# Attention denominators with tokens on partitions, and the last norm inside the feed-forward block

## The chip, the cores and the metric

The kernel runs on one core of one Trainium2 chip, in float32 carried through the matrix engine as pairs of high and low parts. The metric is device microseconds (us) of one execution. Before the change three runs gave a median of 2854.69 us (2854.20 to 2859.28). PE is the matrix engine (TensorE), DVE is VectorE, ACT is ScalarE, POOL is GpSimd, and SP issues most of the DMAs. PSUM is the accumulator memory that PE writes; SBUF is the on-chip memory that all engines share.

## The reference, cut to what matters

One encoder layer is applied to 512 + 1024 = 1536 tokens of width 1024:

- normalise, and one input projection to attention's q, k and v (8 query heads, 2 key heads, width 64), the mLSTM's q, k, v, o and gates, and two merge gates;
- attention in blocks of 512 queries: softmax over all keys of the token's own sequence, `o = sum(p * v) / sum(p)`, where p is the exponential of the score less the query's maximum;
- the mLSTM branch, the merge, the output projection, a norm and a residual, which give x1;
- the gated feed-forward part: `u = h @ w_up`, a convolution and gelu on one half, times the other half, `y = act @ w_down` (2816 to 1024), and last `x1 + rmsnorm(y, norm_ffn_post)`.

## The kernel before

The stages stand one after another, each a block in which every engine has its own list of instructions, ordered by semaphores. Every product of two float32 matrices is three matmuls (`mm3`, lines 77 to 79: high by high, high by low, low by high) of 128 x 128 by 128 x 512.

**Attention (`attention`).** A unit is one head's 512 queries; there are 24. A step is 256 keys of it: eight units have two steps and sixteen have four, 80 steps in all. All engines walk over the same slots, one per step, PE two steps ahead with the scores. In slot i PE does: part of the input projection (`project`, the filling work, about 14 matmuls in a slot); `turn_top` for the unit that starts three slots later; `weigh(i)`, the four products of probabilities and v; more projection; `scores(i+2)`, four matmuls; for a unit that ended in slot i-1, `sums`; and `piece`, products for the row maxima of the next unit, in between more projection. DVE does in slot i: `keep_lo(i+1)` (the low half of the probabilities, L819), then for a unit that ended in slot i-2 `invert` and `normalise`, for one that ends now `fold`, then the low half of a projection weight (L497), the maxima (`reduce`, L804 and L806; `top`, L815), and `add_halves`. POOL adds the probabilities up (L723). ACT takes the exponentials.

The denominators: `fold` leaves 128 x 512 partial sums, keys on partitions. `sums` multiplies them by a 128 x 128 matrix of ones into the bank pDen, which so holds each query's sum on every partition, and DVE takes the reciprocal of 64 x 512 of it (L842) and multiplies (L849). pDen is also where `turn_top` turns the maxima (128 tokens on partitions) into a row. So before it turns, PE waits for all reciprocals so far:

```python
for u in starting(i + 3):
    if sums_done:
        pe.wait_ge(inverted, sums_done)
    turn_top(u)
```

The pieces for the maxima go to the two banks of pM in turn.

**Feed-forward (`ffn`).** A loop runs over the 22 slices of 128 of the inner width. For each, PE makes the gate products, the down products of the slice before (12 token tiles of 128, two halves of 512 each), and the val products. DVE splits weights into halves, runs convolution and activation in three chunks of 512 tokens, and adds each down product to y_sum (L2072). After the last slice PE waits for all three chunks, and makes the last down products.

**Last norm (`final_norm`).** A block of its own behind the loop: per token tile ACT squares and sums y_sum (L2226) and takes the root (L2230), DVE takes the reciprocal (L2242), scales and multiplies by the gain (L2245, 128 x 1024), and adds x1 (L2250, 128 x 1024). SP loads x1 four tiles ahead and stores y.

Of the kernel before, what the change touches and what calls it, by code (L numbers as in the profile page):

```python
# [24 lines left out]
F32 = mybir.dt.float32  # L25
# [499 lines left out]
def attention(nc, k):  # L525

    with ExitStack() as ctx:
# [35 lines left out]
        ones = sb("att_ones", [P, P], F32R)  # L563
# [4 lines left out]
        o_half, o_sum, o_out = sb("o_half", [H2, CH]), sb("o_sum", [H2, CH]), sb("o_out", [H2, 2, CH])  # L568
        top2, tops = sb("att_top2", [P, 4, 2]), sb("att_tops", [P, 4, P])
        rinv = sb("att_rinv", [H2, CH])  # L570
# [4 lines left out]
        g_ones = sb("gate_ones", [R, 2 * CH])  # L575
# [14 lines left out]
        summed, inverted, normed = sem("p_summed"), sem("inverted"), sem("o_normed")  # L590
# [24 lines left out]
        def pieces_until(i):  # L615
            return sum(len(x) for x in PIECES[:i + LEAD])

# [7 lines left out]
        def _(sp):  # L625
# [47 lines left out]
            for i in slots():  # L673
# [14 lines left out]
                for u in ending(i - 2):  # L688
                    store_a(u)
# [36 lines left out]
        def _(act):  # L726
# [14 lines left out]
            def keep_top(u):  # L741
                act.wait_ge(m_turned, u + 1)
                act.wait_ge(q_in[u % 3], 48 * (u // 3 + 1))
                act.activation(q_m[H2:H2 + 1, u % 3, :], pD[H2:H2 + 1, :], ACT.Copy).then_inc(m_kept, 1)
# [50 lines left out]
        def _(dve):  # L795
            def reduce(u, p):
                n = KT[u] // 4
                qb, s = p // n, p % n
                at = BEGUN[u] + p
                dve.wait_ge(pieced, at + 1)  # L800
                if n == 1:
                    if u and p == 0:
                        dve.wait_ge(m_turned, u)
                    dve.tensor_reduce(tops[:, qb, H2:H2 + 1], pM[:, at % 2, :], AX_X, ALU.max).then_inc(reduced, 1)  # L804
                else:
                    dve.tensor_reduce(top2[:, qb, s:s + 1], pM[:, at % 2, :], AX_X, ALU.max).then_inc(reduced, 1)  # L806
# [25 lines left out]
            def add_halves(u):  # L832
                dve.wait_ge(halved, u + 1)
                if u:
                    dve.wait_ge(normed, u)
                dve.tensor_tensor(o_sum[:, :], pO[0:H2, :], o_half[:, :], ALU.add).then_inc(o_added, 1)

            def invert(u):
                dve.wait_ge(summed, u + 1)
                if u:  # L840
                    dve.wait_ge(normed, u)
                dve.reciprocal(rinv[:, :], pD[0:H2, :]).then_inc(inverted, 1)  # L842

            def normalise(u):
                dve.wait_ge(inverted, u + 1)
                dve.wait_ge(o_added, u + 1)
                if u >= 2:
                    dve.wait_ge(a_out[u % 2], 16 * (u // 2))
                dve.tensor_tensor(o_out[:, u % 2, :], o_sum[:, :], rinv[:, :], ALU.mult).then_inc(normed, 1)  # L849
# [39 lines left out]
            for i in slots():  # L889
                if i + 1 >= 0 and i + 1 < NS:  # L890
                    keep_lo(i + 1)
                for u in ending(i - 2):
                    invert(u)
                    normalise(u)
# [24 lines left out]
        def _(pe):  # L919
# [7 lines left out]
            def piece(u, p):  # L927
# [7 lines left out]
                if at >= 2:  # L935
                    pe.wait_ge(reduced, at - 1)
                k0 = SEG_OF_CHUNK[c][0] * P + s * CH
                pe.matmul(pM[:, at % 2, :], q_st[:, u % 3, qb * P:(qb + 1) * P], k_st[:, k0:k0 + CH],  # L938
                          start=True, stop=True).then_inc(pieced, 1)

            def turn_top(u):
                pe.wait_ge(topped, u + 1)
                for qb in range(4):
                    last = pe.transpose(pD[:, qb * P:(qb + 1) * P], tops[:, qb, :], k.ident[:, :])
                last.then_inc(m_turned, 1)
# [28 lines left out]
            def sums(u):  # L974
                pe.wait_ge(fold_split, u + 1)
                pe.matmul(pD[:, :], ones[:, :], s_hi[:, :], start=True, stop=False)
                pe.matmul(pD[:, :], ones[:, :], s_lo[:, :], start=False, stop=True).then_inc(summed, 1)
# [10 lines left out]
            tops_done = sums_done = 0  # L988
            for i in slots():
                due = DUE[i + LEAD]  # L990
                project(due - 2 * (due // 3))
                for u in starting(i + 3):
                    if sums_done:
                        pe.wait_ge(inverted, sums_done)
                    turn_top(u)
                    tops_done += 1
# [5 lines left out]
                for u in ending(i - 1):  # L1002
                    pe.wait_ge(m_kept, tops_done)
                    sums(u)
                    sums_done += 1
# [6 lines left out]
            sums(NU - 1)  # L1012
            pe.wait_ge(exped, 2 * NS)
# [916 lines left out]
def ffn(nc, k, h2_hi, h2_lo, y_sum):  # L1930
# [4 lines left out]
    with ExitStack() as ctx:  # L1935
# [5 lines left out]
        def sem(name):  # L1941
# [22 lines left out]
                                                            sem("act_h"), sem("act_l"), sem("y_summed"))  # L1964
        start_at_one(nc, used)
# [7 lines left out]
        last_f = NFF - 1  # L1973

# [5 lines left out]
        def _(sp):  # L1980
# [20 lines left out]
            with sp.Fori(1, NFF // 2) as i:  # L2001
                three(2 * i, 0)
                three(2 * i + 1, 1)

        @block.vector
        def _(dve):
# [91 lines left out]
            add_down(last_f)  # L2098

        @block.scalar  # L2100
        def _(act):
# [20 lines left out]
            with act.Fori(0, NFF) as f:  # L2122
                copy_gate(f)
                gelus(f)

        @block.tensor
        def _(pe):
# [42 lines left out]
            down_products(last_f)  # L2170

def final_norm(nc, k, y_sum):

    with ExitStack() as ctx:
        def sb(name, shape, dt=F32):
            return ctx.enter_context(nc.sbuf_tensor(name, shape, dt))

        used = []  # L2180

        def sem(name):
            used.append(ctx.enter_context(nc.semaphore(name)))
            return used[-1]

        RING = 4
        gain, x_t, y_t = sb("f_gain", [P, D]), sb("f_x1", [P, RING, D]), sb("f_y", [P, RING, D])
        squares, stat = sb("f_sq", [P, D]), sb("f_stat", [P, 3, RING])
        gain_in, x_in = sem("f_gain_in"), [sem(f"f_x1_in{b}") for b in range(RING)]
        squared, rooted, inverted, scaled, added = sem("f_squared"), sem("f_rooted"), sem("f_inverted"), sem("f_scaled"), sem("f_added")  # L2190
        out = [sem(f"y_out{b}") for b in range(RING)]
        start_at_one(nc, used)
        block = ctx.enter_context(nc.Block())

        def tiles(eng, body):
            with eng.Fori(0, NT // RING) as i:  # L2196
                for b in range(RING):
                    body(RING * i + b, b, i)

        @block.sync  # L2200
        def _(sp):
            sp.dma_start(gain[:, :], k.norm_ffn_post.partition_broadcast(P)).then_inc(gain_in, 16)
            for b in range(RING):
                sp.dma_start(x_t[:, b, :], k.x1[b * P:(b + 1) * P, :]).then_inc(x_in[b], 16)

            def store(t, b):
                sp.wait_ge(added, t + 2)
                sp.dma_start(k.y[bass.ds(t * P, P), :], y_t[:, b, :]).then_inc(out[b], 16)

            with sp.Fori(0, NT // RING - 1) as i:  # L2210
                for b in range(RING):
                    t = RING * i + b
                    store(t, b)
                    sp.dma_start(x_t[:, b, :], k.x1[bass.ds((t + RING) * P, P), :]).then_inc(x_in[b], 16)
            for b in range(RING):
                store(NT - RING + b, b)
            for b in range(RING):
                sp.wait_ge(out[b], 16 * (NT // RING) + 1)

        @block.scalar  # L2220
        def _(act):
            act.sem_inc(inverted, RING - 1)

            def statistics(t, b, i):
                act.wait_ge(rooted, t + 1)
                act.activation(squares[:, :], y_sum[:, bass.ds(t, 1), :].rearrange("p a n -> p (a n)"), ACT.Square,  # L2226
                               accum_out=stat[:, 0, b:b + 1]).then_inc(squared, 1)
                act.wait_ge(squared, t + 2)
                act.wait_ge(inverted, t + 1)
                act.activation(stat[:, 1, b:b + 1], stat[:, 0, b:b + 1], ACT.Sqrt, scale=1.0 / D,  # L2230
                               bias=k.eps[:, 0:1]).then_inc(rooted, 1)

            tiles(act, statistics)

        @block.vector
        def _(dve):
            dve.wait_ge(gain_in, 17)
            dve.wait_ge(inverted, RING)

            def finish(t, b, i):  # L2240
                dve.wait_ge(rooted, t + 2)
                dve.reciprocal(stat[:, 2, b:b + 1], stat[:, 1, b:b + 1]).then_inc(inverted, 1)  # L2242
                dve.wait_ge(inverted, t + RING + 1)  # L2243
                dve.wait_ge(out[b], 16 * i + 1)  # L2244
                dve.scalar_tensor_tensor(out=y_t[:, b, :], in0=y_sum[:, bass.ds(t, 1), :].rearrange("p a n -> p (a n)"),  # L2245
                                         scalar=stat[:, 2, b:b + 1], in1=gain[:, :],
                                         op0=ALU.mult, op1=ALU.mult).then_inc(scaled, 1)
                dve.wait_ge(scaled, t + 2)
                dve.wait_ge(x_in[b], 16 * (i + 1) + 1)  # L2249
                dve.tensor_tensor(y_t[:, b, :], y_t[:, b, :], x_t[:, b, :], ALU.add).then_inc(added, 1)  # L2250

            tiles(dve, finish)
# [46 lines left out]
def encoder_block(nc, x, norm_mix_pre, w_in, b_if, q_norm, k_norm, mlstm_norm_w, w_attn_o, w_mlstm_o, w_out,  # L2299
# [18 lines left out]
    with ExitStack() as ctx:  # L2318
# [22 lines left out]
        with ExitStack() as second:  # L2341
# [4 lines left out]
            final_norm(nc, k, y_sum)  # L2346
# [41 lines left out]
```

## Time and profile before

| | |
|---|---|
| median of three runs | 2854.69 us |
| profiled execution | 2859.45 us |
| its span, first to last instruction | 2857.6 us |
| PE busy | 2483.2 us (87%) |
| DVE busy | 1786.3 us (63%) |
| ACT busy | 885.8 us (31%) |
| POOL busy | 497.1 us (17%) |
| mean granted TensorE clock | 0.934 |

The busy time of an engine counts its instructions and not the waits before them. A group of instructions names its line, its engine, what it writes and reads, its count, its busy time and the mean of one, and the idle time of its engine just before such instructions with what ended it. A granted clock of 1.0 is 2.4 GHz and 0.5 is 1.2 GHz. A matmul's duration contains its run through the pipeline; what it costs in a stream is the distance from start to start.

### The profile page before, as it was taken

What the parts mean: (1) busy time and instruction counts of PE and PEld (TensorE: products, weight loads), DVE (VectorE), ACT (ScalarE), POOL (GpSimd) and SP (SyncE); (2) the same over time, 40 slices, a digit from 0 to 9 for tenths busy, and PEclk for the clock granted to TensorE, in tenths of its full rate; (3) what the DMA queues carried; (4) which work ended last, traced back from release to release, by engine and by line L of the source; (5) the groups of instructions that cost most, each with busy time, mean ns of one, the idle gap of its engine ahead of it and who ended that gap; (6) DMA issues with size and microseconds to landing.
All of it is one profiled execution on the core that took longest, in us unless ns stands there. A gap on an engine that the chain in (4) does not pass through costs nothing. (4 is left out here: it accounts for less than half of the span.)

```text
span 2857.6 us, 32937 instructions
## 1 busy us (share of the span) xinstructions
PE 2483.2 (87%) x11024; PEld 2034.7 (71%) x11024; DVE 1786.3 (63%) x2308; ACT 885.8 (31%) x1395; POOL 497.1 (17%) x430
## 2 busy tenths in 40 slices
PE   5948778878886999997597988999999999999993
PEld 4836666657664878876485776888888888888882
DVE  4626777777764666665534553757576666656577
ACT  2314434434443554544410331111212111111113
POOL 1521222222323544443221000000000000000000
PEclk9968889989997999998798998999999999999996
DMA  6774224323217454532354431111101011111104
GB/s 179 200 195 119 80 70 132 104 69 116 81 54 223 115 177 116 158 96 88 128 182 147 138 116 52 38 29 35 31 22 42 24 37 29 37 29 37 29 15 184
DMA packets 286224, 268.20 MB, mean 94 GB/s; under 512 B 21672, under 2 KB 228776, under 8 KB 286128
## 3 DMA queue, kind: packets, MB, share of 16 engines
q1 hardware_dynamic: 281376, 253.18, 29.7%
q10 hardware_dynamic: 4752, 13.83, 1.2%
q8 instruction: 49, 0.80, 0.1%
q14 instruction: 47, 0.39, 0.0%
HBM read 197.70 MB, written 69.26 MB: 93 GB/s over the span
## 5 line engine op out<-in xcount | busy, mean ns | idle before, releaser
L2072 DVE TENSOR_TENSOR y_sum<-y_sum,pVal 128x512 f32<-128x512 f32 x252 | 171.5, 687 | 208.6 <-PE pVal L79 208.6
L77 PE MATMUL pG<-h2T_hi,wg_hi 128*128 128x512 f32 x528 | 206.5, 391 | 11.2 <-DVE wg_lo L2019 11.2
L78 PE MATMUL pG<-h2T_hi,wg_lo 128*128 128x512 f32 x528 | 206.3, 391 | 0.0
L79 PE MATMUL pG<-h2T_lo,wg_hi 128*128 128x512 f32 x528 | 206.3, 391 | 0.0
L77 PE MATMUL pVal<-h2T_hi,wv_hi 128*128 128x512 f32 x528 | 205.4, 389 | 0.0
L78 PE MATMUL pVal<-h2T_hi,wv_lo 128*128 128x512 f32 x528 | 205.4, 389 | 0.0
L79 PE MATMUL pVal<-h2T_lo,wv_hi 128*128 128x512 f32 x528 | 205.4, 389 | 0.0
L723 POOL TENSOR_TENSOR p_sum<-p_sum,probs 128x1024 f32<-128x1024 f32 x56 | 137.0, 2446 | 379.9 <-ACT probs L733 379.9
L1201 POOL TENSOR_TENSOR w_sum<-w_sum,w_all 128x512 f32<-128x512 f32 (+3 forms) x128 | 149.5, 1168 | 240.9 <-DVE w_all L1306 219.2
L77 PE MATMUL pZ_a<-hT_hi_a,win_hi_a 128*128 128x512 f32 x384 | 158.0, 412 | 31.5 <-DVE win_lo_a L497 27.6
L2117 ACT ACT_TABLE_LOAD x22 | 28.2, 1283 | 477.1 <-DVE conv L2052 477.1
L2072 DVE TENSOR_TENSOR y_sum<-y_sum,pD 128x512 f32<-128x512 f32 x252 | 172.3, 687 | 0.6 <-PE pD L79 0.6
L77 PE MATMUL pZ_m<-hT_hi_m,win_hi_m 128*128 128x512 f32 x384 | 159.4, 415 | 6.6 <-DVE win_lo_m L497 6.3
L78 PE MATMUL pZ_a<-hT_hi_a,win_lo_a 128*128 128x512 f32 x384 | 156.5, 407 | 0.0
L79 PE MATMUL pZ_a<-hT_lo_a,win_hi_a 128*128 128x512 f32 x384 | 155.5, 405 | 0.0
L78 PE MATMUL pZ_m<-hT_hi_m,win_lo_m 128*128 128x512 f32 x384 | 154.3, 402 | 0.0
L79 PE MATMUL pZ_m<-hT_lo_m,win_hi_m 128*128 128x512 f32 x384 | 153.9, 401 | 0.0
L806 DVE TENSOR_REDUCE att_top<-pM 128x1 f32<-128x512 f32 x128 | 86.7, 689 | 96.5 <-PE pM L938 96.5
L819 DVE TENSOR_TENSOR p_lo<-probs,p_hi 128x1024 fp32r<-128x1024 f32 x80 | 130.6, 1632 | 10.7 <-ACT p_hi L739 9.7
L733 ACT ACTIVATE probs<-pS 128x512 f32<-128x512 f32 x160 | 87.5, 595 | 156.3 <-PE pS L956 156.2
L497 DVE TENSOR_TENSOR win_lo_m<-win_raw_m,win_hi_m 128x1024 fp32r<-128x1024 f32 x48 | 67.5, 1406 | 97.4 <-ACT win_hi_m L493 97.4
L77 PEld LDWEIGHTS pG<-h2T_hi,wg_hi 128*128 128x128 f32 x528 | 99.8, 189 | 32.4 <-DVE wg_lo L2019 11.6
(260 smaller groups left out, 6272.4 us busy)
## 6 DMA issues: line engine op xcount, KB each, us to landing
win_raw_a<-in_w_in SPq DMA_DIRECT2D x48, 512.0 KB, 4.2
win_raw_m<-in_w_in SPq DMA_DIRECT2D x48, 512.0 KB, 4.2
ffn_raw<-in_w_up SPq DMA_DIRECT2D x44, 512.0 KB, 3.9
zT_scratch<-z_st_a SPq DMA_DIRECT2D x48, 256.0 KB, 4.4
zT_scratch<-z_st_m SPq DMA_DIRECT2D x48, 256.0 KB, 4.4
a_T<-zT_scratch SPq DMA_DIRECT2D x16, 768.0 KB, 8.6
ffn_raw<-in_w_down SPq DMA_DIRECT2D x22, 512.0 KB, 4.4
m_raw<-zT_scratch SPq DMA_DIRECT2D x36, 256.0 KB, 3.1
```

The costliest lines, as they stand in the source:

```text
L77: pe.matmul(out, w_hi, x_hi, start=first, stop=False, **kw)
L78: pe.matmul(out, w_lo, x_hi, start=False, stop=False, **kw)
L79: return pe.matmul(out, w_hi, x_lo, start=False, stop=last, **kw)
L497: dve.tensor_tensor(self.w_lo[:, g % 2], self.raw[:, g % 2], self.w_hi[:, g % 2].bitcast(F32), ALU.subtract).then_inc(self.split, 1)
L723: pool.tensor_tensor(acc[:, u % 2, :], acc[:, u % 2, :], probs[:, i % 2, :], ALU.add).then_inc(added_up, 1)
L733: act.activation(probs[:, i % 2, a * CH:(a + 1) * CH], pS[:, a, :], ACT.Exp).then_inc(exped, 1)
L806: dve.tensor_reduce(top2[:, qb, s:s + 1], pM[:, at % 2, :], AX_X, ALU.max).then_inc(reduced, 1)
L819: dve.tensor_tensor(p_lo[:, i % 3, :], probs[:, i % 2, :], p_hi[:, i % 3, :].bitcast(F32), ALU.subtract).then_inc(lo_done, 1)
L1201: pool.tensor_tensor(w_sum[:, j % 2, d, cols], w_sum[:, j % 2, d, cols], w_all[:, x % RING, cols], ALU.add).then_inc(added_up, 1)
L2072: dve.tensor_tensor(y_sum[:, t, cols], y_sum[:, t, cols], down_bank(2 * t + h), ALU.add).then_inc(summed, 1)
L2117: act.activation(gelu[:, :], conv[:, :], ACT.Gelu_apprx_tanh, bias=b).then_inc(gelu_done, 1)
```

## The change

In attention:

- `sums` now takes the partial sums as the stationary operand, 128 queries at a time, and two columns of ones as the moving one: eight matmuls with 128 x 2 results in place of two with 128 x 512. The sums lie with queries on partitions, four columns.
- `invert` takes the reciprocal of 128 x 4, and a new multiplication with ones spreads it to 128 x 512 in SBUF (`rwide`).
- A new `turn_inverse` on PE, one slot later, turns that into pDen by four transposes; `normalise` comes one slot later, behind it, and reads pDen. `sums` waits for the normalise of the unit before.
- `turn_top` no longer writes pDen. It takes its place in the order of the pieces, in the two banks of pM; a piece or a turn waits for the reader of the one two places before it (`wait_bank`). The wait for `inverted` before it, and that for `m_kept` before `sums`, are gone.
- `o_sum` has two buffers, and SP's store of a unit comes a slot later.

In the feed-forward block: `final_norm` is gone and its work stands in `ffn`. The last down products are made tile by tile, both halves in a pair of banks (pG's first two, or pD's), and wait only for their own chunk of the activation. DVE adds both halves at once, and scales two tiles behind. POOL adds x1. SP loads x1 into the space of h2_hi and stores from y_sum.

```diff
             def invert(u):
                 dve.wait_ge(summed, u + 1)
+                dve.reciprocal(rinv[:, :], pD[:, 0:8].rearrange("p (q e) -> p q e", e=2)[:, :, 0]).then_inc(inverted, 1)
+                dve.wait_ge(inverted, u + 1)
                 if u:
-                    dve.wait_ge(normed, u)
-                dve.reciprocal(rinv[:, :], pD[0:H2, :]).then_inc(inverted, 1)
+                    dve.wait_ge(r_turned, u)
+                dve.tensor_tensor(rwide[:, :, :], wide_ones, rinv[:, :].unsqueeze(2).to_broadcast([P, 4, P]),
+                                  ALU.mult).then_inc(widened, 1)
...
             def turn_top(u):
                 pe.wait_ge(topped, u + 1)
+                wait_bank(pe, M_AT["turn", u])
                 for qb in range(4):
-                    last = pe.transpose(pD[:, qb * P:(qb + 1) * P], tops[:, qb, :], k.ident[:, :])
+                    last = pe.transpose(pM[:, turn_bank(u), qb * P:(qb + 1) * P], tops[:, qb, :], k.ident[:, :])
                 last.then_inc(m_turned, 1)
...
             def sums(u):
                 pe.wait_ge(fold_split, u + 1)
-                pe.matmul(pD[:, :], ones[:, :], s_hi[:, :], start=True, stop=False)
-                pe.matmul(pD[:, :], ones[:, :], s_lo[:, :], start=False, stop=True).then_inc(summed, 1)
+                if u:
+                    pe.wait_ge(normed, u)
+                for qb in range(4):
+                    cols = slice(qb * P, (qb + 1) * P)
+                    pe.matmul(pD[:, 2 * qb:2 * qb + 2], s_hi[:, cols], ones[:, :], start=True, stop=False)
+                    last = pe.matmul(pD[:, 2 * qb:2 * qb + 2], s_lo[:, cols], ones[:, :], start=False, stop=True)
+                last.then_inc(summed, 1)
+
+            def turn_inverse(u):
+                pe.wait_ge(widened, u + 1)
+                for qb in range(4):
+                    last = pe.transpose(pD[:, qb * P:(qb + 1) * P], rwide[:, qb, :], k.ident[:, :])
+                last.then_inc(r_turned, 1)
...
                 for u in starting(i + 3):
-                    if sums_done:
-                        pe.wait_ge(inverted, sums_done)
                     turn_top(u)
...
                 for u in ending(i - 1):
-                    pe.wait_ge(m_kept, tops_done)
                     sums(u)
-                    sums_done += 1
+                for u in ending(i - 2):
+                    turn_inverse(u)
...
+        @block.gpsimd
+        def _(pool):
+            for t in range(NT):
+                pool.wait_ge(scaled, t + 1)
+                pool.wait_ge(x_in[t % XR], 16 * (t // XR + 1))
+                row = halves(y_sum[:, t, :])
+                pool.tensor_tensor(row, row, x_row(t), ALU.add).then_inc(added, 1)
...
+            def last_sum(t):
+                dve.wait_ge(downed, NDT * last_f + t + 2)
+                dve.wait_ge(summed, NDT * last_f + 1)
+                row = halves(y_sum[:, t, :])
+                dve.tensor_tensor(row, row, pair(t), ALU.add).then_inc(done_t, 1)
+
+            def scale(t):
+                dve.wait_ge(rooted, t + 1)
+                dve.reciprocal(stat[:, 2, t:t + 1], stat[:, 1, t:t + 1]).then_inc(inverted, 1)
+                dve.wait_ge(inverted, t + 1)
+                dve.scalar_tensor_tensor(out=y_sum[:, t, :], in0=y_sum[:, t, :], scalar=stat[:, 2, t:t + 1],
+                                         in1=post[:, :], op0=ALU.mult, op1=ALU.mult).then_inc(scaled, 1)
+
+            dve.wait_ge(post_in, 16)
+            for t in range(NT + 2):
+                if t < NT:
+                    last_sum(t)
+                if t >= 2:
+                    scale(t - 2)
...
+            for t in range(NT):
+                pe.wait_ge(act_l, NCH * last_f + t // 4 + 2)
+                if t >= 2:
+                    pe.wait_ge(done_t, t - 1)
+                else:
+                    pe.wait_ge(summed, NDT * last_f + 1)
```

## Rows read from the trace of the kernel before

**Rows 1.** Stretches: length; busy PE, PEld, DVE, ACT, POOL; granted clock; DMA share; GB/s.

```profile
235.50:851.00 615.50, 502.61 (x2002) 397.43 (x2002) 462.44 (x443) 270.45 (x376) 159.28 (x79) 0.90 0.31 88
317.30:321.20 3.90, 3.88 (x11) 3.24 (x12) 1.22 (x2) 2.13 (x3) 0.00 (x0) 0.50 0.15 34
321.30:347.00 25.70, 20.80 (x90) 16.41 (x88) 23.50 (x23) 12.05 (x17) 8.25 (x4) 0.96 0.39 108
2815.00:2858.00 43.00, 0.00 (x0) 0.00 (x0) 31.08 (x36) 25.02 (x42) 0.00 (x0) 0.52 0.82 305
```

**Rows 2.** Groups of instructions by line, all of the span.

```profile
L944 PE MATMUL pDen<-ident,att_tops 128*128 128x128 f32 x96 | 23.7, 393 | 94.1 <-DVE att_rinv L842 89.6 <-DVEq L811 4.6
L842 DVE RECIPROCAL att_rinv<-pDen 64x512 f32<-64x512 f32 x24 | 80.2, 3342 | 0.5 <-PE pDen L977 0.5
L830 DVE TENSOR_TENSOR p_fold_lo<-p_fold,p_fold_hi 128x512 fp32r<-128x512 f32 x24 | 16.6, 692 | 0.8
L285 DVE TENSOR_TENSOR h_lo<-pT,h_hi 128x1024 fp32r<-128x1024 f32 x12 | 14.6, 1218 | 1.7 <-ACT h_hi L213 1.7
```

**Rows 3.** Timeline of PE, two turns of the maxima: start, duration, idle before.

```profile
317.32 1.12 PE L944 MATMUL pDen<-ident,att_tops 128*128 128x128 f32 x4 [5.30 <-DVE att_rinv L842]
...
321.22 0.40 PE L955 MATMUL pS<-q_stack,k_stack 128*128 128x512 f32 x1
...
322.15 0.40 PE L938 MATMUL pM<-k_stack,q_stack 128*128 128x512 f32 x1
...
379.04 1.11 PE L944 MATMUL pDen<-ident,att_tops 128*128 128x128 f32 x4 [6.86 <-DVE att_rinv L842]
```

**Rows 4.** Timeline of DVE around the first of these turns.

```profile
310.74 2.12 DVE L815 TENSOR_TENSOR att_tops<-att_top 128x4 f32<-128x4 f32 x1
312.79 1.21 DVE L819 TENSOR_TENSOR p_lo<-probs,p_hi 128x1024 fp32r<-128x1024 f32 x1
313.92 3.34 DVE L842 RECIPROCAL att_rinv<-pDen 64x512 f32<-64x512 f32 x1
```

**Rows 5.** Timeline of PE: two of sixteen matmuls with two columns; four transposes.

```profile
920.53 0.25 PE L1439 MATMUL pMV<-m_ones,w_sum_lo 128*128 128x2 f32 x1
...
921.64 0.25 PE L1439 MATMUL pMV<-m_ones,w_sum_lo 128*128 128x2 f32 x1
...
241.29 0.60 PE L944 MATMUL pDen<-ident,att_tops 128*128 128x128 f32 x4
241.65 0.47 PE L969 MATMUL pO<-p_hi,v_both 128*128 128x512 f32 x1
```

**Rows 6.** Timelines of POOL and DVE where their instructions meet.

```profile
118.42 0.89 POOL L353 TENSOR_TENSOR rot_b<-qk_n,sin 128x320 f32<-128x320 f32 x1
118.73 1.66 DVE L280 SCALAR_TENSOR_TENSOR x_scaled<-x_t,stat,mix_gain 128x1024 f32<-128x1024 f32 x1
119.39 1.74 POOL L357 TENSOR_TENSOR qk_r<-rot_a,rot_b 128x320 f32<-128x320 f32 x1
...
323.13 2.41 POOL L723 TENSOR_TENSOR p_sum<-p_sum,probs 128x1024 f32<-128x1024 f32 x1 [10.28 <-ACT probs L733]
323.50 0.69 DVE L806 TENSOR_REDUCE att_top<-pM 128x1 f32<-128x512 f32 x1 [0.23 <-PE pM L938]
324.18 2.44 DVE L819 TENSOR_TENSOR p_lo<-probs,p_hi 128x1024 fp32r<-128x1024 f32 x1
```

**Rows 7.** Timelines of ACT and DVE from the last activation to the end.

```profile
2794.71 0.69 DVE L2059 TENSOR_TENSOR act_lo<-gelu,act_hi 128x512 fp32r<-128x512 f32 x1 [0.70 <-ACT act_hi L2120]
2816.42 1.28 ACT L2226 ACT_TABLE_LOAD   x1 [21.73 <-PEq L2263]
2820.17 0.29 ACT L2230 ACTIVATE f_stat<-f_stat,eps 128x1 f32<-128x1 f32 x1
2821.00 1.28 DVE L2245 SCALAR_TENSOR_TENSOR f_y<-y_sum,f_stat,f_gain 128x1024 f32<-128x1024 f32 x1 [0.24 <-DVE f_stat L2242]
2853.27 1.23 DVE L2250 TENSOR_TENSOR f_y<-f_y,f_x 128x1024 f32<-128x1024 f32 x1
```

More of the change, by code:

```diff
@@ L562, in attention @@
         v_both = sb("v_both", [P, NT, 2 * H2], F32R)
-        ones = sb("att_ones", [P, P], F32R)
+        ones = sb("att_ones", [P, 2], F32R)
         probs = sb("probs", [P, 2, 2 * CH])
@@ L567, in attention @@
         s_f, s_hi, s_lo = sb("p_fold", [P, CH]), sb("p_fold_hi", [P, CH], F32R), sb("p_fold_lo", [P, CH], F32R)
-        o_half, o_sum, o_out = sb("o_half", [H2, CH]), sb("o_sum", [H2, CH]), sb("o_out", [H2, 2, CH])
+        o_half, o_sum, o_out = sb("o_half", [H2, CH]), sb("o_sum", [H2, 2, CH]), sb("o_out", [H2, 2, CH])
         top2, tops = sb("att_top2", [P, 4, 2]), sb("att_tops", [P, 4, P])
-        rinv = sb("att_rinv", [H2, CH])
+        rinv, rwide = sb("att_rinv", [P, 4]), sb("att_rwide", [P, 4, P])
         R = 64
@@ L574, in attention @@
         gi, gf, t0, t1 = (sb(f"gate_{n}", [R, TOK]) for n in ("gi", "gf", "t0", "t1"))
-        g_ones = sb("gate_ones", [R, 2 * CH])
+        g_ones = sb("gate_ones", [P, 2 * CH])
+        wide_ones = g_ones[:, 0:4 * P].rearrange("p (q t) -> p q t", t=P)
         pS = ctx.enter_context(nc.psum_tensor("pS", [P, 2, CH], F32))
@@ L589, in attention @@
         folded, fold_hi, fold_split = sem("p_folded"), sem("fold_hi"), sem("fold_split")
-        summed, inverted, normed = sem("p_summed"), sem("inverted"), sem("o_normed")
+        summed, inverted, widened = sem("p_summed"), sem("inverted"), sem("r_widened")
+        r_turned, normed = sem("r_turned"), sem("o_normed")
         halved, o_added, a_out = sem("o_halved"), sem("o_added"), [sem(f"a_out{b}") for b in range(2)]
@@ L616, in pieces_until, with turn_bank, piece_bank, wait_bank @@
             return sum(len(x) for x in PIECES[:i + LEAD])
+        M_ORDER = []
+        for i in range(-LEAD, NS):
+            M_ORDER += [("turn", u) for u in range(NU) if FIRST[u] == i + 3]
+            M_ORDER += [("piece", BEGUN[u] + p) for u, p in PIECES[i + LEAD]]
+        M_AT = {x: m for m, x in enumerate(M_ORDER)}
+        def turn_bank(u):
+            return M_AT["turn", u] % 2
+        def piece_bank(at):
+            return M_AT["piece", at] % 2
+        def wait_bank(pe, m):
+            if m >= 2:
+                kind, n = M_ORDER[m - 2]
+                pe.wait_ge(m_kept if kind == "turn" else reduced, n + 1)
         SCANS_FROM = 10
@@ L687, in _ @@
                     load_v(1, 1)
-                for u in ending(i - 2):
+                for u in ending(i - 3):
                     store_a(u)
@@ L743, in keep_top @@
                 act.wait_ge(q_in[u % 3], 48 * (u // 3 + 1))
-                act.activation(q_m[H2:H2 + 1, u % 3, :], pD[H2:H2 + 1, :], ACT.Copy).then_inc(m_kept, 1)
+                act.activation(q_m[H2:H2 + 1, u % 3, :], pM[H2:H2 + 1, turn_bank(u), :], ACT.Copy).then_inc(m_kept, 1)
             def halve(u):
@@ L803, in reduce @@
                         dve.wait_ge(m_turned, u)
-                    dve.tensor_reduce(tops[:, qb, H2:H2 + 1], pM[:, at % 2, :], AX_X, ALU.max).then_inc(reduced, 1)
+                    dve.tensor_reduce(tops[:, qb, H2:H2 + 1], pM[:, piece_bank(at), :], AX_X, ALU.max).then_inc(reduced, 1)
                 else:
-                    dve.tensor_reduce(top2[:, qb, s:s + 1], pM[:, at % 2, :], AX_X, ALU.max).then_inc(reduced, 1)
+                    dve.tensor_reduce(top2[:, qb, s:s + 1], pM[:, piece_bank(at), :], AX_X, ALU.max).then_inc(reduced, 1)
             def top(u):
@@ L833, in add_halves @@
                 dve.wait_ge(halved, u + 1)
-                if u:
-                    dve.wait_ge(normed, u)
-                dve.tensor_tensor(o_sum[:, :], pO[0:H2, :], o_half[:, :], ALU.add).then_inc(o_added, 1)
+                if u >= 2:
+                    dve.wait_ge(normed, u - 1)
+                dve.tensor_tensor(o_sum[:, u % 2, :], pO[0:H2, :], o_half[:, :], ALU.add).then_inc(o_added, 1)
             def invert(u):
                 dve.wait_ge(summed, u + 1)
+                dve.reciprocal(rinv[:, :], pD[:, 0:8].rearrange("p (q e) -> p q e", e=2)[:, :, 0]).then_inc(inverted, 1)
+                dve.wait_ge(inverted, u + 1)
                 if u:
-                    dve.wait_ge(normed, u)
-                dve.reciprocal(rinv[:, :], pD[0:H2, :]).then_inc(inverted, 1)
+                    dve.wait_ge(r_turned, u)
+                dve.tensor_tensor(rwide[:, :, :], wide_ones, rinv[:, :].unsqueeze(2).to_broadcast([P, 4, P]),
+                                  ALU.mult).then_inc(widened, 1)
             def normalise(u):
-                dve.wait_ge(inverted, u + 1)
+                dve.wait_ge(r_turned, u + 1)
                 dve.wait_ge(o_added, u + 1)
@@ L848, in normalise @@
                     dve.wait_ge(a_out[u % 2], 16 * (u // 2))
-                dve.tensor_tensor(o_out[:, u % 2, :], o_sum[:, :], rinv[:, :], ALU.mult).then_inc(normed, 1)
+                dve.tensor_tensor(o_out[:, u % 2, :], o_sum[:, u % 2, :], pD[0:H2, :], ALU.mult).then_inc(normed, 1)
             def scan(out_t, data1, op1, n):
@@ L893, in _ @@
                     invert(u)
+                for u in ending(i - 3):
                     normalise(u)
@@ L934, in piece @@
                     pe.wait_ge(kv_in[0 if c == 0 else 1], 48 * (g + 1))
-                if at >= 2:
-                    pe.wait_ge(reduced, at - 1)
+                wait_bank(pe, M_AT["piece", at])
                 k0 = SEG_OF_CHUNK[c][0] * P + s * CH
-                pe.matmul(pM[:, at % 2, :], q_st[:, u % 3, qb * P:(qb + 1) * P], k_st[:, k0:k0 + CH],
+                pe.matmul(pM[:, piece_bank(at), :], q_st[:, u % 3, qb * P:(qb + 1) * P], k_st[:, k0:k0 + CH],
                           start=True, stop=True).then_inc(pieced, 1)
@@ L987, in _ @@
             pe.wait_ge(fixed_v, 2)
-            tops_done = sums_done = 0
             for i in slots():
@@ L992, in _ @@
                 for u in starting(i + 3):
-                    if sums_done:
-                        pe.wait_ge(inverted, sums_done)
                     turn_top(u)
-                    tops_done += 1
                 if i >= 0:
@@ L1012, in _ @@
             sums(NU - 1)
+            turn_inverse(NU - 1)
             pe.wait_ge(exped, 2 * NS)
@@ L1964, in ffn, with fresh @@
                                                             sem("act_h"), sem("act_l"), sem("y_summed"))
+        XR = 4
+        post = sb("f_gain", [P, D])
+        stat = sb("f_stat", [P, 3, NT])
+        def fresh(name):
+            return ctx.enter_context(nc.semaphore(name))
+        post_in, x_in = fresh("f_gain_in"), [fresh(f"f_x1_in{b}") for b in range(XR)]
+        done_t, squared, rooted = fresh("f_summed"), fresh("f_squared"), fresh("f_rooted")
+        inverted, scaled, added, y_out = fresh("f_inverted"), fresh("f_scaled"), fresh("f_added"), fresh("y_out")
         start_at_one(nc, used)
@@ L1973, in ffn, with halves, x_row, pair @@
         last_f = NFF - 1
+        def halves(a):
+            return a.rearrange("p (h n) -> p h n", n=CH)
+        def x_row(t):
+            return h2_hi[:, 2 * (t % XR):2 * (t % XR) + 2, 0:CH].bitcast(F32)
+        def pair(t):
+            return pG[:, 0:2, :] if t % 2 == 0 else pD[:, :, :]
         def down_bank(j):
@@ L2003, in _, with load_x1 @@
                 three(2 * i + 1, 1)
+            def load_x1(t):
+                sp.dma_start(x_row(t), halves(k.x1[t * P:(t + 1) * P, :])).then_inc(x_in[t % XR], 16)
+            sp.dma_start(post[:, :], k.norm_ffn_post.partition_broadcast(P)).then_inc(post_in, 16)
+            sp.wait_ge(vald, NCH * last_f + 2)
+            for t in range(XR):
+                load_x1(t)
+            for t in range(NT):
+                sp.wait_ge(added, t + 1)
+                sp.dma_start(k.y[t * P:(t + 1) * P, :], y_sum[:, t, :]).then_inc(y_out, 16)
+                if t + XR < NT:
+                    load_x1(t + XR)
+            sp.wait_ge(y_out, 16 * NT)
+        @block.gpsimd
[5 more added lines that the diff above has]
+                pool.tensor_tensor(row, row, x_row(t), ALU.add).then_inc(added, 1)
         @block.vector
@@ L2097, in _ @@
             step(NFF // 2 - 1, 1, last=True)
-            add_down(last_f)
+            def last_sum(t):
[15 more added lines that the diff above has]
+                    scale(t - 2)
         @block.scalar
@@ L2124, in _ @@
                 gelus(f)
+            act.wait_ge(wsplit, 3 * NFF + 1)
+            for t in range(NT):
+                act.wait_ge(done_t, t + 1)
+                if t:
+                    act.wait_ge(squared, t)
+                act.activation(raw[:, 0, :], y_sum[:, t, :], ACT.Square,
+                               accum_out=stat[:, 0, t:t + 1]).then_inc(squared, 1)
+                act.wait_ge(squared, t + 1)
+                act.activation(stat[:, 1, t:t + 1], stat[:, 0, t:t + 1], ACT.Sqrt, scale=1.0 / D,
+                               bias=k.eps[:, 0:1]).then_inc(rooted, 1)
         @block.tensor
@@ L2169, in _ @@
                 val_products(f)
[L2170 to L2252, printed above, removed]
@@ new lines, in _ @@
+            pe.wait_ge(wsplit, 3 * last_f + 4)
+            pe.wait_ge(gate_copied, NCH * NFF + 1)
+            for t in range(NT):
+                pe.wait_ge(act_l, NCH * last_f + t // 4 + 2)
[3 more added lines that the diff above has]
+                    pe.wait_ge(summed, NDT * last_f + 1)
+                for h in range(D // CH):
+                    cols = slice(h * CH, (h + 1) * CH)
+                    last = mm3(pe, pair(t)[:, h, :], act_hi[:, t * P:(t + 1) * P], act_lo[:, t * P:(t + 1) * P],
+                               d_hi[:, cols], d_lo[:, cols], True, True)
+                last.then_inc(downed, 1)
@@ L2345, in encoder_block @@
             ffn(nc, k, h2_hi, h2_lo, y_sum)
-            final_norm(nc, k, y_sum)
 def rotary_tables():
```

## The prediction, made before the changed kernel ran

> **What bounds the kernel now.** I read the groups of instructions first, sorted by the idle time before them. One stands out: PE sat idle for 94.1 us before the 24 turns of the maxima, 89.6 us of it until a reciprocal on DVE had ended, and that reciprocal of 64 x 512 takes 3.34 us [rows 2]. Next I looked at the timelines of PE and DVE around one such turn. The turn begins at 317.32, after 5.30 us in which PE did nothing [rows 3]. The maxima that it turns had been ready at 310.74 + 2.12 = 312.86; what still ran was the next low half and then the reciprocal, until 317.26 [rows 4]. So PE waits for a bank, not for its data. Last I looked at the stretches: in attention PE is busy for 502.6 of 615.5 us and DVE for 462.4, at a mean clock of 0.90; right behind the stall the granted clock is 0.50 for 3.9 us, and 0.96 in the 26 us after [rows 1]. PE bounds attention, with stops of that one kind in it.
>
> The end is a second, smaller place: from 2815 on PE does nothing, and DVE runs 31 of 43 us [rows 1]. The last activation ends at 2795.40, the first table load of the norm begins at 2816.42, and the last addition of x1 ends at 2854.50, 3.1 us before the span of 2857.6 [rows 7].
>
> **The stall in attention.** It goes. What is late next is the maxima. At the turn shown PE is free at 317.32 - 5.30 = 312.02 and they come at 312.86: 0.84 us remain of 5.30. An L815 of 2.12 us for 128 x 4 is long beside the 0.69 of a maximum over 512 columns [rows 6], so I take it for a slow one. Bounds: 0 to 0.84 for each of 20 turns; I take 0.15, 3 us. Gain 89.6 - 3 = 87 us.
>
> **The clock.** PE spends 3.9 us at half clock behind the stall shown, which costs half of it, 1.95 us [rows 1]. For 20 stalls the bounds are 0 and 39 us. PE's other stops (615.5 - 502.6 - 89.6 = 23 us [rows 1, 2]) and new small ones remain and may keep the clock down; I take 24 us.
>
> **What PE gets to do in addition.** Eight matmuls with two columns stand (921.64 - 920.53) / 10 = 0.11 us apart, 0.89 us; four transposes take 241.65 - 241.29 = 0.36 us [rows 5]. Two matmuls of 512 columns go: four of these and their successor begin at 321.22 and 322.15, 0.23 each, 0.47 us for two [rows 3]. Net 0.78 us in each of 24 units, 19 us; PE is the bound, so I count it in full. Bounds: 0 (if PE would wait anyway) and twice that at half clock, 38.
>
> **DVE.** The reciprocal goes from 512 columns to 4: 80.2 us become at most 24 x 0.2 = 5 (3.34 us by 4/512 and a fixed part below 0.2 us). The spreading is new: 128 x 512 from SBUF, as L830, 0.69 us, 17 us in all [rows 2]. Normalise reads PSUM instead of SBUF, at no cost. DVE is relieved of 58 us, which lies beside PE's work and is worth only what it makes earlier.
>
> **The new wait.** PE now waits in slot e+2 (e: the unit's last) for the spread reciprocal. Behind it on PE's list are the pieces and the projection, and DVE's next maxima wait for the pieces. In the turn shown: DVE could begin the reciprocal at 313.92, and ends the spreading 0.2 + 0.69 and some 0.2 for semaphores later, at 315.0. PE, released at 312.96, does the turn (0.36), four products, three projections and four scores (11 x 0.23 = 2.5) and is there at 315.9. It does not wait. At the longest stall, 6.86 us [rows 3], DVE is late by 1.56 us more against PE, and PE would wait for about 0.7 to 1.5 us. Bounds: 0, and 24 x 2.4 = 58 us if each spreading met POOL's addition of 2.41 us (below). Most stalls are shorter than 5.3 us (89.6/20 = 4.5), so I stay near the lower end: 15 us, with what the other edits may delay. Those are the banks of pM shared with the turn (a piece waits for ACT's copy of the row, which ACT makes while PE weighs and scores, over 2 us), the wait of `sums` for the normalise before it (in units of two steps it is due early in the same slot, behind one low half), and SP's later store, past which loads of weights queue as they did.
>
> Attention: -87 - 24 + 19 + 15 = -77 us. Its very end has one reciprocal of 3.34 us with nothing beside it; there some 1.4 us are won by the shorter chain of 1.5 us with 0.4 us more on PE.
>
> **The end.** PE makes the first two tiles while DVE is still at the activation, so DVE adds tile 0 from 2795.40 (1.22 us, as L285 [rows 2]) to 2796.6. ACT's first root costs two table loads, 2816.42 to 2820.46, 4.04 us, and from there to the end of the first scaling are 1.82 us [rows 7]: 2802.5. Then POOL adds x1 to 128 x 1024, 2.41 us as in L723 [rows 6].
>
> What decides is how POOL and DVE meet. L819 was issued at 324.18 with POOL's addition running until 325.54, and ended at 326.62, 1.08 us after POOL; alone it takes 1.21. L280, the same kind as the new scaling, was issued at 118.73, POOL's L353 ended at 119.31, and L280 ended 1.08 us later; and POOL's L357, issued at 119.39, ended at 121.13, about 0.87 us after L280's end near 120.3. L806, which reads PSUM, ran beside POOL at its usual 0.69 [rows 6]. So scaling and addition take turns, and the sums from PSUM run beside: a tile costs 2.41 + 1.08 + 0.1 = 3.6 us. Twelve tiles end at 2802.6 + 2.4 + 11 x 3.6 = 2844.6, and the store takes 2857.6 - 2854.5 = 3.1 us more: 2847.7, 10 us earlier than now. Bounds: 2.5 us a tile if POOL alone paced it (22 us won), 4.2 with longer handovers (3 won). The new PE, ACT and SP work is hidden: a tile's six matmuls (1.4 us, 2.8 at half clock), ACT's 1.5 us (4.04 less two table loads of 1.28) and a load issued four tiles ahead all fit into 3.6 us.
>
> The Trainium skill, SBUF — State Buffer, section Who interferes with whom, says that a VectorE instruction with two SBUF inputs and a GpSimd instruction that reads SBUF exclude each other for their whole length. By that rule the move to POOL gives a pitch of 3.6 us where engines that only queue would have 2.5, and the sum is -88 instead of -100; the rows above agree with it.
>
> **Sum.** -77 - 1 - 10 = -88 us against the profiled execution's 2859.45, that is 2771. That execution was 4.8 us above the median of the runs, 2854.69; on the median's scale 2767, and I say 2768.
>
> **Rivals.**
> - *The stall moves on* (slots on DVE, products waiting for o_sum): half of the stall comes back at other lines, at which DVE is late. For it: DVE is busy for 23.5 of 25.7 us in the stretch behind the turn [rows 1], a tight list in order. Against it: 3.34 of these are the reciprocal. Attention then gains half, 38 us: 2806.
> - *POOL alone paces the end*: 12 us more, 2756. Against it: L280 [rows 6].
> - *The turned inverse becomes the stall* (slower): PE waits at the new transposes in each unit for the reciprocal and the spreading. With w us each, and no clock regained, attention changes by -87 + 19 + 24 w; with the 11 us of the ends the whole is slower from w = 3.3 us on. With 5 us, today's stall: +41, 2896. For it: the same order of DVE decides. Against it: DVE's part is 0.9 us instead of 3.3, and PE gets there 2.9 us later.
> - *The wait is not the bank's*: then the turn stays as late as it was, the extra work costs 19, and the end gives 10: 2864. Against it: the turn begins 0.06 us after the reciprocal's end, 4.5 us after its data.
>
> **Chances.** Forecast 0.65, stall moves on 0.19, POOL paces 0.10, inverse stalls 0.04, not the bank 0.02. 0.2% of this time is 5.7 us, about what a measurement can tell from no change. Forecast and the next two are faster, 0.94; slower 0.04; the rest 0.02 near no change. Range 2738 to 2806: below, all of the clock and no new waits (-15 -15) with part of POOL's 12; above, the case of the stall that moves on.
>
> **What would show it.** Right: no idle time on PE before the turned maxima beyond 5 us in all; the reciprocal at 0.2 us; attention's stretch from 615 to about 540 us with a clock of 0.94 or more; POOL's additions and DVE's scalings in turn, 3.6 us apart, and the span's end 52 us after the last activation instead of 62. Wrong: idle time of tens of us before the new transposes, or before the weighing; scalings of 1.28 us that run while POOL adds.

## The result and the profile after

The changed kernel takes 2728.8 us (2728.3 to 2731.2) beside 2857.0 for the one before: a ratio of 0.955, 95% interval 0.953 to 0.957. The direction was right, the time lies 9 us below the range, and the gain is 128 us where 87 were forecast.

Two stretches of the changed kernel answer to [rows 1]: attention from its first to its last weighing, and the end from the last activation on.

```profile
233.50:731.50 498.00, 482.92 (x2233) 388.84 (x2232) 388.02 (x466) 270.47 (x376) 161.80 (x79) 0.99 0.38 109
2677.50:2727.50 50.00, 16.01 (x61) 10.55 (x60) 43.40 (x37) 18.45 (x37) 28.37 (x12) 0.84 0.60 210
```

Attention fell from 615.5 to 498.0 us, and PE is busy for 97% of it at a clock of 0.99. DVE's busy time in it fell from 462 to 388 us. The end fell from 62.2 us (2795.4 to 2857.6 [rows 7]) to 49.9 (2677.6 to 2727.5). Together that is 130 us, the difference of the two spans; what lies ahead of attention and what lies between the two stretches are each within 2 us of before.

The groups of the whole span that answer to [rows 2], and the group of the weighing:

```profile
L969 PE MATMUL pM<-ident,att_tops 128*128 128x128 f32 x96 | 15.7, 288 | 3.4 <-DVEq L832 2.9 <-DVE att_tops L836 0.5
L1012 PE MATMUL pDen<-ident,att_rwide 128*128 128x128 f32 x96 | 14.7, 275 | 3.5 <-DVE att_rwide L865 3.5
L994 PE MATMUL pO<-p_hi,v_both 128*128 128x512 f32 x160 | 66.2, 414 | 6.1 <-DVE o_sum L857 5.4
L861 DVE RECIPROCAL att_rinv<-pDen 128x4 f32<-128x4 f32 x24 | 4.1, 172 | 0.9 <-PE pDen L1006 0.9
```

The 94.1 us of idle time before the turn are 3.4, PE waits before the new transposes for 3.5 us in all, and the reciprocal takes 0.17 us instead of 3.34.

For the end of the program, DVE's and POOL's timelines show two tiles:

```profile
2683.28 2.38 POOL L2081 TENSOR_TENSOR y_sum<-y_sum,h2T_hi 128x1024 f32<-128x1024 f32 x1 [1259.64 <-DVE y_sum L2187]
2684.44 2.30 DVE L2187 SCALAR_TENSOR_TENSOR y_sum<-y_sum,f_stat,f_gain 128x1024 f32<-128x1024 f32 x1
2686.66 1.21 DVE L2181 TENSOR_TENSOR y_sum<-y_sum,pG 128x1024 f32<-128x1024 f32 x1
2686.82 2.38 POOL L2081 TENSOR_TENSOR y_sum<-y_sum,h2T_hi 128x1024 f32<-128x1024 f32 x1 [1.16 <-DVE y_sum L2187]
```

The scaling is issued while POOL adds, and ends 1.08 us after it (2685.66 to 2686.74); the sum from PSUM runs beside POOL at its usual 1.21. Tiles are 3.54 us apart.

### The profile page after: what moved, and what is told of

It is laid out like the page before. It is cut to its first block and busy times, and to the rows that moved or that the text cites. A ratio compares the mean times of both kernels' runs of the same rounds, so it can differ in the third digit from the quotient of the medians.

```text
span 2727.5 us, 33259 instructions
## 1 busy us (share of the span) xinstructions
PE 2467.3 (90%) x11264; PEld 2029.7 (74%) x11264; DVE 1705.6 (63%) x2308; ACT 880.5 (32%) x1390; POOL 527.8 (19%) x442
## 5 line engine op out<-in xcount | busy, mean ns | idle before, releaser
L2150 DVE TENSOR_TENSOR y_sum<-y_sum,pVal 128x512 f32<-128x512 f32 x240 | 163.4, 688 | 206.0 <-PE pVal L79 206.0
L2081 POOL TENSOR_TENSOR y_sum<-y_sum,h2T_hi 128x1024 f32<-128x1024 f32 x12 | 28.4, 2364 | 1272.4 <-DVE y_sum L2187 1272.4
L2150 DVE TENSOR_TENSOR y_sum<-y_sum,pD 128x512 f32<-128x512 f32 x240 | 164.2, 688 | 0.0
```

The costliest lines, as they stand in the source:

```text
L2081: pool.tensor_tensor(row, row, x_row(t), ALU.add).then_inc(added, 1)
L2150: dve.tensor_tensor(y_sum[:, t, cols], y_sum[:, t, cols], down_bank(2 * t + h), ALU.add).then_inc(summed, 1)
```

## The experiments

Stretches are from the first to the last weighing; "idle" is such a stretch less PE's busy time in it. A ratio is to the kernel before on the same chip: 2857.0 us beside the changed kernel, 2863.3 beside the next four, 2858.5 beside the last four. Times from different groups are best compared by their ratios.

| kernel | time, us | ratio to before | stretch | idle |
|---|---|---|---|---|
| before | | 1 | 615.5 | 113 |
| changed | 2728.8 | 0.955 (0.953 to 0.957) | 497.9 | 15 |
| attention's part alone | 2740.8 | 0.957 (0.956 to 0.959) | 497.5 | 15 |
| last norm's part alone | 2850.5 | 0.996 (0.994 to 0.997) | 613.0 | 113 |
| banks alone | 2811.3 | 0.982 (0.980 to 0.983) | 567.6 | 78 |
| short reciprocal alone | 2768.5 | 0.966 (0.965 to 0.968) | 524.4 | 34 |
| small matmuls twice | 2757.7 | 0.965 (0.963 to 0.966) | 525.3 | 12 |
| unused reciprocal behind | 2800.5 | 0.980 (0.978 to 0.981) | 567.7 | 59 |
| unused reciprocal ahead | 2857.0 | 0.999 (0.998 to 1.000) | 622.5 | 94 |
| gain in PSUM | 2719.0 | 0.951 (0.949 to 0.953) | | |

**The two parts.** One kernel has the change in `attention` alone, one that in `ffn` with `final_norm` gone.

> Only the attention part of the change, the last norm as before. If the two parts don't touch each other: attention's stretch (first to last weighing) falls from 615 to 498 us as in the whole change, and the time is 12 us above it, about 2741. If some of the gain in attention came from the rest of the program (another layout, other code), the stretch stays above 510 us.

> Only the last norm behind the last products, attention as before. By the sum of the two parts: 12 us below before, about 2843, with scalings and POOL's additions in turn, 3.5 us a tile. If the end gains only since attention changed: nothing, 2855.

Both as expected: attention's stretch is 497.5 us with the first part alone, and with the second alone the end takes 49.8 us (2795.1 to 2844.9) with tiles 3.5 us apart. The gains of 0.0428 and 0.0044 sum to 0.0472, beside 0.045 for both; with these intervals no effect of one part on the other shows.

**Banks alone.** The kernel before with the change's order of banks, and the old denominators:

```diff
-                    last = pe.transpose(pD[:, qb * P:(qb + 1) * P], tops[:, qb, :], k.ident[:, :])
+                    last = pe.transpose(pM[:, turn_bank(u), qb * P:(qb + 1) * P], tops[:, qb, :], k.ident[:, :])
...
             def sums(u):
                 pe.wait_ge(fold_split, u + 1)
+                if u:
+                    pe.wait_ge(inverted, u)
...
                 for u in starting(i + 3):
-                    if sums_done:
-                        pe.wait_ge(inverted, sums_done)
                     turn_top(u)
```

> Attention as before, but the maxima are turned in pM's banks as in the change, and sums waits for the reciprocal of the unit before; the reciprocal stays 64 x 512 long (3.34 us). Theory (the shared bank was the fault): PE's idle time before the turns falls from 94 us to under 10, attention's stretch to about 515 to 525 us, the time to about 2760. Rival (DVE's 80 us of reciprocals are the fault, whichever bank): DVE's list is then the limit, PE's idle time comes back before the weighing, the maxima or the projection's weights, the stretch stays at 560 us or more, and the time at 2800 or more.

The idle time at the turns did go (in the stretch 1.7 us, beside 89.6 before), and the rival still won: idle time came back elsewhere. PE's groups in the stretch of this kernel:

```profile
L77 PE MATMUL pZ_a<-hT_hi_a,win_hi_a 128*128 128x512 f32 x362 | 149.0, 412 | 33.7 <-DVE win_lo_a L497 27.9 <-DMA hT_lo_a<-hT_lo_scratch 5.8
L986 PE MATMUL pO<-p_hi,v_both 128*128 128x512 f32 x160 | 70.6, 441 | 31.2 <-DVE o_sum L853 30.8
L954 PE MATMUL pM<-k_stack,q_stack 128*128 128x512 f32 x150 | 60.2, 408 | 11.1 <-DVE att_top L823 10.8
L961 PE MATMUL pM<-ident,att_tops 128*128 128x128 f32 x88 | 13.6, 277 | 1.7 <-DVE att_tops L832 1.7
```

How it comes back is seen at the turn of [rows 3], here in PE's and DVE's timelines:

```profile
313.16 0.66 PE L961 MATMUL pM<-ident,att_tops 128*128 128x128 f32 x4 [0.16 <-DVE att_tops L832]
314.16 3.34 DVE L859 RECIPROCAL att_rinv<-pDen 64x512 f32<-64x512 f32 x1
317.54 2.52 DVE L866 TENSOR_TENSOR o_out<-o_sum,att_rinv 64x512 f32<-64x512 f32 x1
319.99 1.21 DVE L497 TENSOR_TENSOR win_lo_a<-win_raw_a,win_hi_a 128x1024 fp32r<-128x1024 f32 x1
321.25 0.79 PE L77 MATMUL pZ_a<-hT_hi_a,win_hi_a 128*128 128x512 f32 x1 [3.73 <-DVE win_lo_a L497]
```

Counted from the first weighing PE turns 2.6 us earlier than before, 0.16 us after it became free, and 8 us later it waits 3.73 us for the weights. These stand behind the reciprocal and the normalise on DVE's list; the normalise itself took 2.52 us here, beside a mean of 0.78 before. DVE is busy for 470 of the 568 us: its list is not full, but it is in order, and what stands behind a long instruction comes late.

**Short reciprocal alone.** The change's denominators, with their two buffers of `o_sum`, but the maxima are still turned in pDen:

```diff
                 for u in starting(i + 3):
+                    if sums_done:
+                        pe.wait_ge(inverted, sums_done)
+                    if inv_done:
+                        pe.wait_ge(normed, inv_done)
                     turn_top(u)
```

> The denominators as in the change (short reciprocal, spreading, turned inverse), but the maxima are still turned in pDen, and PE waits before that for the reciprocals so far. Theory (the bank): PE still waits at each turn, for 3.1 us less each: some 20 x 1.4 = 28 us of idle time there, attention's stretch 530 to 545, the time about 2780. Rival (DVE's time): almost all of the gain is there, the stretch is 515 or less and the time 2750 or less.

The wait at the turn is still there, 23.6 us for the 28 expected, so the bank by itself costs about what the theory says. But the stretch was 524 us and the time 2768.5, better than either figure of that theory and short of the rival's. Other waits of PE had fallen as well: as in the changed kernel, 5.4 us are left of the weighing's wait for o_sum and 0.2 of the wait for the weights, beside 11.0 and 7.6 before. PE's group of the turns, in the stretch:

```profile
L969 PE MATMUL pDen<-ident,att_tops 128*128 128x128 f32 x88 | 15.1, 297 | 23.6 <-DVE att_rinv L861 23.6
```

**DVE's load by itself.** The changed kernel with a reciprocal that nothing uses, behind the spreading in one kernel, ahead of the short reciprocal in another:

```diff
+                dve.reciprocal(g_ones[H2:P, CH:2 * CH], g_ones[H2:P, CH:2 * CH]).then_inc(spared, 1)
```

> The changed kernel, with a reciprocal of 64 x 512 (3.34 us) that nothing uses on DVE behind each unit's spreading: DVE's time as before the change, the banks and the short chain as after it. Theory (after the stall DVE's list is the next limit, so both parts of the change are needed): PE's idle time comes back before the weighing, the projection and the maxima, attention's stretch is 555 to 575 us as in the run with the banks alone, the time about 2795. Rival (what made the banks alone slow was that sums waited for the long reciprocal): the stretch stays under 520 us, the time under 2750.

> As the run before it, but the unused reciprocal stands ahead of the short one, so that the spread inverse comes 3.34 us later as well. PE reaches the new transposes a median of 1.2 us after the spreading's end in the changed kernel; by these distances it would wait 50 us in all there. Theory (these waits come on top of DVE's late list): 20 to 50 us slower than the run with the load alone, 2815 to 2845. Rival (PE is late anyway then, so that the distances grow with DVE's load): the same time as that run within 10 us.

Behind: 567.7 us, about the stretch with the banks alone. (That they agree to a tenth is chance: PE's idle time is 59 us in one and 78 in the other.) No other engine waits for that reciprocal, and the rest of the change stands, the two buffers of `o_sum` too; so DVE's time by itself costs 70 us of attention. Of these 44 are idle time of PE; for the other 26 PE is busy for longer (509 us for 483), at a mean clock of 0.94 where the changed kernel has 0.99. PE's groups in the stretch:

```profile
L77 PE MATMUL pZ_a<-hT_hi_a,win_hi_a 128*128 128x512 f32 x362 | 149.4, 413 | 19.7 <-DVE win_lo_a L497 15.7 <-DMA hT_lo_a<-hT_lo_scratch 3.7
L998 PE MATMUL pO<-p_hi,v_both 128*128 128x512 f32 x160 | 71.1, 444 | 26.1 <-DVE o_sum L858 25.6
```

Ahead: 56 us more, somewhat over the 20 to 50 that were expected, and the kernel is back at the time before the change. The new waits do not simply come on top: before the weighing 12.7 us are left of 26.1, before the projection 4.4 of 19.7. PE's group of the new transposes, in the whole span:

```profile
L1016 PE MATMUL pDen<-ident,att_rwide 128*128 128x128 f32 x96 | 23.3, 388 | 73.8 <-DVE att_rwide L869 73.7
```

That is the prediction's slower rival brought about: 73.8 / 24 = 3.1 us a unit, together with the load on DVE, take away all of the gain, where the rival had put the limit at 3.3. The changed kernel is at 0.15.

**The added PE work.** Each `for qb in range(4)` of `sums` and `turn_inverse` runs twice.

> The changed kernel, with the eight small matmuls of each unit's sums and the four transposes of its inverse made twice (the second round writes the same). It adds 8 x 0.11 + 4 x 0.09 = 1.25 us of PE to each of 24 units. Theory (PE is the bound of attention now): all of it counts, +30 us, about 2759. Rival (they fit into PE's waits, which is why the gain was larger than forecast): +10 us or less, under 2740.

The stretch, which holds 23 of the 24 units, grew by 27.4 us of the 28.8 added in it. So PE's added work counts nearly in full; that it hid in PE's waits is not why the gain was larger than forecast.

**The end.** The gain is copied once to PSUM:

```diff
+            act.activation(pV[:, 0:2, :], halves(post[:, :]), ACT.Copy).then_inc(gain_kept, 1)
...
-                dve.scalar_tensor_tensor(out=y_sum[:, t, :], in0=y_sum[:, t, :], scalar=stat[:, 2, t:t + 1],
-                                         in1=post[:, :], op0=ALU.mult, op1=ALU.mult).then_inc(scaled, 1)
+                row = halves(y_sum[:, t, :])
+                dve.scalar_tensor_tensor(out=row, in0=row, scalar=stat[:, 2, t:t + 1],
+                                         in1=pV[:, 0:2, :], op0=ALU.mult, op1=ALU.mult).then_inc(scaled, 1)
...
+            dve.wait_ge(gain_kept, 1)
```

> The changed kernel, with the gain of the last norm copied once (by ACT) into two banks of pVal that are free by then, so that DVE's scaling reads one operand from SBUF and one from PSUM instead of two from SBUF. Theory (scaling and POOL's addition exclude each other, since both read two operands from SBUF): the scaling takes its 1.28 us again beside the addition, tiles come 2.5 to 2.6 us apart instead of 3.54, the end is 10 to 12 us earlier, about 2718. Rival (a tile costs 3.5 us because of the handover between the engines, or because POOL slows whatever DVE does): the pitch stays at 3.5 us, and the time at 2729.

As the theory has it. DVE's and POOL's timelines:

```profile
2701.18 1.28 DVE L2189 SCALAR_TENSOR_TENSOR y_sum<-y_sum,f_stat,pVal 128x1024 f32<-128x1024 f32 x1
2697.50 7.43 POOL L2082 TENSOR_TENSOR y_sum<-y_sum,h2T_hi 128x1024 f32<-128x1024 f32 x3
2703.70 1.28 DVE L2189 SCALAR_TENSOR_TENSOR y_sum<-y_sum,f_stat,pVal 128x1024 f32<-128x1024 f32 x1
```

Three additions take 7.43 us, 2.48 each, and beside them runs a scaling of 1.28 us, the same operation of the same size that took 2.30. Tiles are 2.5 us apart, and from the last activation to the end it is 38.7 us (2681.5 to 2720.2) instead of 49.9. The Trainium skill, SBUF — State Buffer, section Who interferes with whom, says that a VectorE instruction with at most one SBUF input (outside certain modes) does not contend with GpSimd; this pair of runs agrees, with 2.30 and 1.28 us.

Then that kernel, with DVE's wait for the copy moved to ahead of the first scaling, beside the changed kernel on the same chip:

> The changed kernel itself, beside the next run on the same chip: 0.955 of before.

> The changed kernel with the gain in PSUM as before, and DVE's wait for that copy moved from ahead of its first sum to ahead of its first scaling. By the exclusion of scaling and addition: 11 us below the changed kernel on the same chip, 0.4%, with tiles 2.5 us apart. If the difference between the two was one between chips: the same time.

2726.2 us (0.953 of before, 0.951 to 0.955) and 2717.2 (0.950, 0.948 to 0.952). The medians differ by 9.0 us, a little less than the 11 expected; the intervals of the ratios just overlap, but each of the five times of the second kernel (2715.7 to 2718.8) is below each of the first (2724.5 to 2734.9). In the profiles of the two the end takes 49.8 and 38.3 us, 11.5 less. So it is not a difference between chips. The second is the fastest version that ran.

## Why the prediction was wrong

The failed step is the term for DVE, "DVE is relieved of 58 us, which lies beside PE's work and is worth only what it makes earlier": the sum put what it makes earlier at nothing. The runs showed that PE's old waits for DVE, before the weighing and before the projection's weights, fell by 13 us; without these the time would be 2742, inside the range. How much rests on DVE's list the run with the unused reciprocal behind shows: its 3.34 us a unit cost 70 us of attention. Two more terms were mis-sized: the new waits came to 4 us where 15 were allowed, and the clock gave 36 where 24 were taken. Term by term, in attention's stretch (PE's idle time by what ended it):

| term | forecast | measured |
|---|---|---|
| idle at the turns | -87 | -89.1 |
| other waits of PE, new and old | +15 | -8.7 |
| added PE work | +19 | +16.6 |
| clock | -24 | -36.4 (the rest) |
| sum | -77 | -117.6 |

The groups of the two old waits before the change, and of the second one after it, in the whole span (20 us of the waits for the weights lie ahead of the stretch, in both kernels):

```profile
L969 PE MATMUL pO<-p_hi,v_both 128*128 128x512 f32 x160 | 75.8, 473 | 11.6 <-DVE o_sum L836 11.0
L77 PE MATMUL pZ_a<-hT_hi_a,win_hi_a 128*128 128x512 f32 x384 | 158.0, 412 | 31.5 <-DVE win_lo_a L497 27.6 <-DMA hT_lo_a<-hT_lo_scratch 3.8
L77 PE MATMUL pZ_a<-hT_hi_a,win_hi_a 128*128 128x512 f32 x384 | 155.0, 404 | 23.8 <-DVE win_lo_a L497 19.9 <-DMA hT_lo_a<-hT_lo_scratch 3.7
```

- *The other waits* are 24 of the 41 us missed. New ones came to 4 us where 15 were allowed. Old ones that I left standing fell by 13: before the weighing from 11.0 to 5.4, before the projection's weights from 7.6 to 0.2 in the stretch. Both are waits for DVE, and with the banks alone and with the unused reciprocal behind they are the two largest. So DVE's list was the second limit, just below PE's work. Own banks alone give attention 48 us, the short reciprocal alone 91, both 118 and not 139: each removes part of the same waiting.
- *The clock* is 12 us of them. Before, the granted clock was 0.5 for 122.9 us of the stretch, in 21 periods in which PE was busy for 90.6 us; after, for 6.8 us in two, with PE busy throughout. By the prediction's own measure, half of the busy time at 0.5, that is worth 42 us; the rest in the table is 36, and where the two part is open. I had bounded it at 39 and took 24, because other stops of PE might keep the clock down. They did not: 15 us of idle time in other stops are left, and the mean clock is 0.99.
- *Added PE work*: made a second time it took 27.4 us for 23 units, 1.19 each; less 0.47 for the two matmuls that went, it is 0.72 a unit, 16.6 us.
- *The end* was right in its mechanism. It gained 12.3 us for 10: the pitch was 3.54 for 3.6, and ACT needed one table load for two, since its square ran without one behind the last gelu. One reading in it was off without effect on the sum: L357 ended 0.74 us after L280 (121.13 less 120.39 [rows 6]), not 0.87.
- *Rivals.* "The stall moves on" happens as named, at the weights and o_sum, when the reciprocal keeps its length. I gave it 0.19 on the ground that DVE's list is tight, and did not draw the other conclusion from the same row: that shortening the list takes such waits away. The range reached down to 2738 with all of the clock and no new waits, and had no case in which old waits fall.

## What to carry to other kernels

Where one wait on a second engine stands out, ask what that engine's list costs without the wait: here its own bank alone was worth 48 us, and an instruction of 3.34 us in each unit on DVE's list cost 70 us even where no other engine waited for it. When an engine is not far below the bound (here DVE was busy for 462 us beside PE's 503), price its relief by the waits that it now ends, all of them. And a number per token belongs on partitions before a slow operation: 4 columns instead of 512.

## What the runs showed of the hardware

A reciprocal on DVE takes 3.34 us for 512 columns, 0.17 for 4, and 0.15 for 1 in the last norm. Over 512 columns that is 6.5 ns a column, where an operation on two tensors takes 0.69 us, 1.4 ns a column [rows 2]. A matmul with two columns and a new 128 x 128 stationary operand costs 0.11 us in a stream [rows 5], half of one with 512 columns (0.23 [rows 3]).
